# Float32r in place of float32: the gate products over stacked rounded parts, the folds of the modulations in two passes

## What is computed

```python
mod_ctx = jax.nn.silu(c_ctx) @ w_ada[l] + b_ada[l]            # modulations: 2 rows of 6 * 2048
mod_lat = (jax.nn.silu(c) @ w_ada[l] + b_ada[l])[:, None, :]
...
h = x * (1 + sc1) + sh1
z = h @ w_in
q, k, v, g, a_f, a_b, p = jnp.split(z, [K_OFF, V_OFF, G_OFF, AF_OFF, AB_OFF, P_OFF], axis=-1)
log_a_f = heads(jax.nn.log_sigmoid((a_f @ w_a2[0] + b_a[0]).astype(f32)) / GLA_GATE_TEMP, GLA_DK)
log_a_b = heads(jax.nn.log_sigmoid((a_b @ w_a2[1] + b_a[1]).astype(f32)) / GLA_GATE_TEMP, GLA_DK)
```

## Time and profile before

| | |
|---|---|
| median of 3 runs | 2717.18 us (2715.28 to 2717.35) |
| the profiled execution, its own time | 2721.88 us |
| its span, first to last instruction | 2720.1 us |
| PE busy | 2643.3 us (97%) |
| DVE, ACT, POOL busy | 1424.9, 898.4, 652.8 us (52%, 33%, 24%) |
| stage with gates and folds | about 150 to 610 us of the span |
| mean granted TensorE clock | 0.991 of full speed |

### The profile page before, as it was taken

The page is one execution under the profiler, slowest core; times in us unless marked ns, Lnnn a source line. Parts: engine busy times, 40 slices in busy tenths (PEclk is TensorE's granted clock), DMA queues, the critical chain, the costliest instruction groups (busy, mean ns, idle before and its releaser), DMA issues.

```text
span 2720.1 us, 37395 instructions
## 1 busy us (share of the span) xinstructions
PE 2643.3 (97%) x16040; PEld 2354.7 (87%) x16040; DVE 1424.9 (52%) x1680; ACT 898.4 (33%) x940; POOL 652.8 (24%) x218
## 2 busy tenths in 40 slices
PE   5999999998999999999999999999999999999997
PEld 3787877797988879999999999999999888888875
DVE  5323232346576457655555545555566354444578
ACT  4333333332311154333333333333333333333343
POOL 0000000000000001344443444344434333333440
PEclk9999999999999989999999999999999999999998
DMA  9775757422463142332233323332334645464566
GB/s 378 281 277 209 272 207 255 153 90 91 176 218 118 64 159 80 108 108 88 93 108 108 96 86 106 108 103 84 101 108 158 239 174 213 174 213 166 208 231 233
DMA packets 179384, 438.11 MB, mean 161 GB/s; under 512 B 9980, under 2 KB 25732, under 8 KB 173076
## 3 DMA queue, kind: packets, MB, share of 16 engines
q1 hardware_dynamic: 176916, 430.48, 45.4%
q10 hardware_dynamic: 2304, 5.24, 0.5%
HBM read 401.83 MB, written 33.85 MB: 160 GB/s over the span
## 4 chain that ended last, share of the span: by engine, by line
PE 62%; DVE 11%; DMA 10%; POOL 10%; issue 4%; ACT 3%; SPq 0%; POOLq 0%; ACTq 0%; DVEq 0%
PE ps L2355 6%; PE ps L2356 6%; PE ps L2357 6%; DMA raw_w<-w_gu_b 5%; PE ps L2278 5%; PE ps L2280 5%; PE ps L2279 5%; PE ps L2031 5%; PE ps L2033 5%; PE ps L2032 5%; POOL raw_w L945 3%; PE ps L2011 3%; DVE w_lo L1666 3%; POOL low L942 2%; POOL raw_w L948 2%
## 5 line engine op out<-in xcount | busy, mean ns | idle before, releaser
L1666 DVE TENSOR_TENSOR w_lo<-raw_w,w_hi 128x1024 fp32r<-128x1024 f32 x264 | 336.6, 1276 | 297.6 <-ACT w_hi L1210 294.7
L1210 ACT ACTIVATE w_hi<-raw_w 128x1024 fp32r<-128x1024 f32 x264 | 270.1, 1054 | 601.0 <-POOL raw_w L951 368.9
L2278 PE MATMUL ps<-x_hi,w_hi 128*128 128x320 f32 x1408 | 435.7, 309 | 1.0 <-DVE w_lo L1666 0.7
L2279 PE MATMUL ps<-x_lo,w_hi 128*128 128x320 f32 x1408 | 435.1, 309 | 0.0
L2280 PE MATMUL ps<-x_hi,w_lo 128*128 128x320 f32 x1408 | 435.1, 309 | 0.0
L942 POOL TENSOR_TENSOR low<-raw_w 128x1024 f32<-128x1024 f32 x41 | 103.7, 2528 | 1098.8 <-DMA raw_w<-w_gu_b 1058.7
L1801 DVE TENSOR_TENSOR x_lo<-low,x_hi 128x2560 fp32r<-128x2560 f32 (+2 forms) x55 | 221.3, 4027 | 262.6 <-ACT x_hi L1303 262.6
L2355 PE MATMUL ps<-w_hi,x_hi 128*128 128x512 f32 x880 | 343.8, 391 | 7.7 <-DVE w_lo L1932 2.8
L2356 PE MATMUL ps<-w_lo,x_hi 128*128 128x512 f32 x880 | 343.1, 390 | 0.0
L2357 PE MATMUL ps<-w_hi,x_lo 128*128 128x512 f32 x880 | 342.9, 390 | 0.0
L2278 PE MATMUL ps<-low_r,w_hi 128*128 128x320 f32 x1072 | 333.0, 311 | 1.5 <-DVE w_lo L1666 1.5
(11 more groups left out here) (238 smaller groups left out, 4362.9 us busy)
## 6 DMA issues: line engine op xcount, KB each, us to landing
raw_w<-w_gu_b SPq DMA_DIRECT2D x180, 512.0 KB, 5.6
low<-w_ada SPq DMA_DIRECT2D x68, 1024.0 KB, 6.9
raw_w<-w_down SPq DMA_DIRECT2D x55, 1024.0 KB, 5.2
low<-hidden_scratch SPq DMA_DIRECT2D x33, 1280.0 KB, 6.0
raw_w<-w_in_b SPq DMA_DIRECT2D x33, 1024.0 KB, 9.1
x_raw<-w_ada SPq DMA_DIRECT2D x25, 1024.0 KB, 15.2
raw_w<-w_out SPq DMA_DIRECT2D x16, 1024.0 KB, 5.1
hidden_scratch<-high SPq DMA_DIRECT2D x44, 320.0 KB, 5.9
```

What stands on the lines that cost most here:

```text
L1210: nc.scalar.activation(weight(0, w), src, ACT.Copy).then_inc(prod_hi, 1)
L1666: nc.vector.tensor_tensor(weight(1, n), src, weight(0, n).bitcast(F32), ALU.subtract).then_inc(prod_split, 1)
L2278: mm(out, wh, version(v, 0, k), start=first and k == 0, stop=False)
L2279: mm(out, wh, version(v, 1, k), start=False, stop=False)
```

## The change

Gates: unit 0's 32 columns are copied twice on POOL beside themselves, so that the unit's product gives `a` on 96 partitions. ACT writes it rounded to float32r (96 rows), and once more unrounded for the middle 32..64 rows; DVE turns rows 32 to 63 into the remainder (`a_split`). The weights `wa` are loaded three times (three DMAs a head) onto 96 partitions of `high`, ACT rounds them (`wa_parts`, line 1165 of the new file), DVE makes the last 32 rows the remainder. So one float32r product over 96 rows is rounded times rounded, remainder times rounded and rounded times remainder. The row of ones is gone; the bias is loaded once as columns (one DMA of 128 x 8 single elements) and added in the DVE minimum and in the ACT absolute value.

Folds: ACT writes the copy of bank 3 rounded, DVE makes the remainder (a new item on DVE for `adarow`), and each fold is two float32r passes with `group_sum_r`. PE waits for `ada_rest` (the remainder) where it waited for `ada_row`.

The core of the diff:

```diff
-        for at, item in ((1, ("wa", h, 0)), (2, ("state", h, 0)), ...
+        for at, item in ((1, ("wa", h, 0)), (3, ("wa_parts", h, 0)), (2, ("state", h, 0)), ...
@@ SyncE
             elif kind == "wa":
                 if a:
-                    x, k = USES["gate", a - 1, 1][0]
-                    sp.wait_ge(filled[x], k + 1)
-                sp.dma_start(low[0:K_ARR, L_WA:L_WA + 256].rearrange("p (d c) -> p d c", d=2),
-                             wa2[:, :, a * DK:(a + 1) * DK]).then_inc(wa_in, 16)
+                    sp.wait_ge(wa_split, a)
+                else:
+                    sp.dma_start(cols(C_BA, 2 * HEADS).rearrange("p (d h) -> p d h", d=2),
+                                 wa2[2 * RANK].rearrange("d (h p) -> p d h", p=P),
+                                 allow_slow_non_contiguous=True).then_inc(ba_in, 16)
+                for i in range(3):
+                    dst = high[32 * i:32 * i + 32, H_WA:H_WA + 256].rearrange("p (d c) -> p d c", d=2)
+                    sp.dma_start(dst, wa2[0:2 * RANK, :, a * DK:(a + 1) * DK]).then_inc(wa_in, 16)
@@ GpSimd
+        pool.wait_ge(raw_in[0], 16)
+        first_unit = raw_w[:, 0, :].rearrange("p (k c) -> p k c", k=KT)
+        for i in (1, 2):
+            nc.gpsimd.tensor_copy(first_unit[:, :, 32 * i:32 * i + 32],
+                                  first_unit[:, :, 0:32]).then_inc(a_copied, 1)
@@ ScalarE
+            if u == 0:
+                act.wait_ge(a_copied, 2)
...
             if kind == "a":
                 for half in range(2):
-                    ins = nc.scalar.activation(half_of(low[0:2 * RANK, L_AT:L_AT + T], half),
-                                               ps[0:2 * RANK, main_bank(n, half), 0:HALF], ACT.Copy)
+                    nc.scalar.activation(half_of(low_r[0:3 * 2 * RANK, L_AT:L_AT + T], half),
+                                         ps[0:3 * 2 * RANK, main_bank(n, half), 0:HALF], ACT.Copy)
+                for half in range(2):
+                    ins = nc.scalar.activation(half_of(low[2 * RANK:4 * RANK, L_E:L_E + T], half),
+                                               ps[2 * RANK:4 * RANK, main_bank(n, half), 0:HALF], ACT.Copy)
...
+            elif kind == "wa_parts":
+                act.wait_ge(wa_in, 48 * (a + 1))
+                if a:
+                    x, k = USES["gate", a - 1, 1][0]
+                    act.wait_ge(filled[x], k + 1)
+                nc.scalar.activation(low_r[0:3 * 2 * RANK, L_WA:L_WA + 256], high[0:3 * 2 * RANK, H_WA:H_WA + 256],
+                                     ACT.Copy).then_inc(wa_rounded, 1)
...
-                nc.scalar.activation(high[:, H_ROW:H_ROW + 512], ps[:, 3, :], ACT.Copy).then_inc(ada_row, 1)
+                nc.scalar.activation(row_parts[0], ps[:, 3, :], ACT.Copy).then_inc(ada_row, 1)
@@ VectorE
+            elif kind == "adarow":
+                if a:
+                    xx, kk = USES["adacol" if ADA[(a - 1) // 4][1] == "col" else "adasum", a - 1, 0][0]
+                    dve.wait_ge(filled[xx], kk + 1)
+                dve.wait_ge(ada_row, a + 1)
+                nc.vector.tensor_tensor(row_parts[1], ps[:, 3, :], row_parts[0].bitcast(F32),
+                                        ALU.subtract).then_inc(ada_rest, 1)
...
+            elif kind == "wa_parts":
+                rows = slice(4 * RANK, 6 * RANK)
+                dve.wait_ge(wa_rounded, a + 1)
+                nc.vector.tensor_tensor(low_r[rows, L_WA:L_WA + 256], high[rows, H_WA:H_WA + 256],
+                                        low_r[rows, L_WA:L_WA + 256].bitcast(F32),
+                                        ALU.subtract).then_inc(wa_split, 1)
...
-                nc.vector.tensor_scalar(lo(L_LA, T), pair(x), 0.0, None, ALU.min).then_inc(gate_split, 1)
+                dve.wait_ge(ba_in, 16)
+                nc.vector.tensor_scalar(lo(L_LA, T), pair(x), gate_bias(a, b), 0.0, ALU.add,
+                                        ALU.min).then_inc(gate_split, 1)
@@ TensorE
                 elif b == 0:
-                    pe.wait_ge(ada_row, a)
+                    pe.wait_ge(ada_rest, a)
...
             elif kind == "gate":
                 x, k = uses[0]
-                pe.wait_ge(zin_evac, 1)
-                pe.wait_ge(ones_row, 1)
-                pe.wait_ge(wa_in, 16 * (a + 1))
+                pe.wait_ge(a_split, 1)
+                pe.wait_ge(wa_split, a + 1)
                 take(x, k)
                 for c, n in ((0, 512), (512, T - 512)):
-                    ins = pair_mm(x, n, c, low[0:K_ARR, L_WA + b * P:L_WA + (b + 1) * P],
-                                  low[0:K_ARR, L_AT + c:L_AT + c + n], True, True)
+                    ins = pair_mm(x, n, c, low_r[0:6 * RANK, L_WA + b * P:L_WA + (b + 1) * P],
+                                  low_r[0:6 * RANK, L_AT + c:L_AT + c + n], True, True)
...
             elif kind == "adasum":
                 x, k = uses[0]
-                pe.wait_ge(ada_row, a + 1)
+                pe.wait_ge(ada_rest, a + 1)
                 take(x, k)
-                mm(pair(x, 512)[0:2, :], group_sum, high[:, H_ROW:H_ROW + 512],
-                   start=True, stop=True).then_inc(filled[x], 1)
+                mm(pair(x, 512)[0:2, :], group_sum_r, row_parts[0], start=True, stop=False)
+                mm(pair(x, 512)[0:2, :], group_sum_r, row_parts[1], start=False, stop=True).then_inc(filled[x], 1)
             elif kind == "adacol":
...
-                    ins = mm(pair(x, 8)[:, 2 * kk:2 * kk + 2], high[:, H_ROW + kk * P:H_ROW + (kk + 1) * P],
-                             group_sum, start=True, stop=True)
+                    for i in range(2):
+                        ins = mm(pair(x, 8)[:, 2 * kk:2 * kk + 2], row_parts[i][:, kk * P:(kk + 1) * P],
+                                 group_sum_r, start=i == 0, stop=i == 1)
```

More of the change, by code:

```diff
@@ L92 @@
 C_COND = C_SUM + 2
-N_PERM = C_COND + 32 * KT
+C_BA = C_COND + 32 * KT
+C_SUMR = C_BA + 2 * HEADS
+N_PERM = C_SUMR + 2
 L_Q, L_K, L_V, L_LA, L_E, L_E3 = 0, 640, 1280, 2560, 3200, 3840
@@ L159 @@
 H_SCORE, H_ROW = 0, 2048
-H_CARRY = 640
-H_RC = 960
+H_CARRY = 320
+H_WA = 640
+H_RC = 896
+H_REST = 1536
 F_A, F_B, F_SIL, F_HF = 0, 640, 960, 1280
@@ L199, in make_schedule @@
         after_k = 4 * (where["k", h, 0] + 1)
-        for at, item in ((1, ("wa", h, 0)), (2, ("state", h, 0)), (2, SLOT), (4, ("gate", h, 0)), (4, SLOT),
+        for at, item in ((1, ("wa", h, 0)), (3, ("wa_parts", h, 0)), (2, ("state", h, 0)), (2, SLOT), (4, ("gate", h, 0)), (4, SLOT),
                          (6, ("vT", h, 0)), (6, SLOT), (6, ("cum", h, 0)), (8, ("score", h, 0)), (8, SLOT),
@@ L334, in backbone @@
     w_down_v = w_down.rearrange("(g k p) (nb c) -> nb g p k c", g=N_DG, k=DG, p=P, nb=4)
-    perm = nc.alloc_sbuf_tensor("perm", [P, N_PERM], F32)
+    with nc.sbuf_tensor("perm", [P, N_PERM], F32) as perm:
+        pass
+    perm_r = nc.alloc_sbuf_tensor("perm_r", [P, N_PERM], F32R)
     with nc.sbuf_tensor("x_raw", [P, 2 * KT * T], F32) as x_raw:
@@ L348, in backbone @@
     low_r = nc.alloc_sbuf_tensor("low_r", [P, LOW], F32R)
-    high = nc.alloc_sbuf_tensor("high", [P, HIGH], F32)
+    with nc.sbuf_tensor("high", [P, HIGH], F32) as high:
+        pass
+    high_r = nc.alloc_sbuf_tensor("high_r", [P, HIGH], F32R)
     ps = nc.alloc_psum_tensor("ps", [P, 8, 512], F32)
@@ L385, in backbone @@
     group_sum = cols(C_SUM, 2)
+    group_sum_r = perm_r[:, C_SUMR:C_SUMR + 2]
+    row_parts = [high_r[:, c:c + 512] for c in (H_ROW, H_REST)]
     mod_col = cols(C_MOD, 64).rearrange("p (s k c) -> p s k c", s=2, c=2)
@@ L397, in backbone, with gate_bias @@
     carry = high[:, H_CARRY:H_CARRY + HALF]
+    def gate_bias(h, d):
+        return cols(C_BA + HEADS * d + h, 1)
     mean_square = cols(C_STAT + 40, TT)
@@ L530, in backbone @@
     drained = [sem("pair_a_drained"), sem("pair_b_drained")]
-    ones_row = sem("ones_row")
+    a_copied = sem("a_copied")
+    a_split = sem("a_split")
+    ba_in = sem("ba_in")
+    wa_rounded = sem("wa_rounded")
+    wa_split = sem("wa_split")
     wa_in = sem("wa_in")
@@ L563, in backbone @@
     ada_row = sem("ada_row")
+    ada_rest = sem("ada_rest")
+    sums_rounded = sem("sums_rounded")
     row_out = sem("row_out")
@@ L972, in split_in @@
             act.wait_ge(raw_in[s], 16 * (u // 2 + 1))
-            if u == 2:
+            if u == 0:
+                act.wait_ge(a_copied, 2)
+            elif u == 2:
                 act.wait_ge(turned, 4 * TT)
@@ L1009, in evac_turned_a @@
                                      ACT.Copy).then_inc(turned_out_a, 1)
+        act.wait_ge(sums_ready, 1)
+        nc.scalar.activation(group_sum_r, group_sum, ACT.Copy).then_inc(sums_rounded, 1)
         for t in range(TT):
@@ L1128, in _ @@
                 act.wait_ge(gate_split, g + 1)
-                nc.scalar.activation(e, pair(x), ACT.Abs).then_inc(drained[x], 1)
+                nc.scalar.activation(e, pair(x), ACT.Abs, bias=gate_bias(a, b)).then_inc(drained[x], 1)
                 act.wait_ge(drained[x], k + 1)
```

(7 more changed lines are left out.)

6 lines of the change are left out of this document (3 added, 3 removed).

## The result

The changed kernel takes 2721.95 us (median of 22 runs, 2717.69 to 2726.14), the kernel before 2717.62 us (22 runs, 2713.28 to 2722.18). I had forecast 2712.3 us, 2707.0 to 2717.5.

A forecast was written before the change was run, and what follows sets the result against it. Between 150 and 600 us TensorE's own work was taken as the bound. Gates save 1.9 us of 7.4 after waits, row folds 3.0, column folds nothing: 4.9 us off 2717.2 gives 2712.3 us, range 2707.0 to 2717.5.

The forecast's parts named there:

- Prices on PE: TensorE cost per step: a gate 0.34 us, saving 0.93; a row fold saves 0.38; a column fold saves nothing.
- My lower end for the column folds: Column folds on TensorE, worst case: passes at 0.15 us cost 0.25 us more a fold, 2.0 in all.
- First gate: PE would wait for the block's remainder on DVE until about 164.0: the gate's saving gone and 0.1 us lost.
- Second and sixth: nothing behind them is close: 0.93 each: Second and sixth gates: no close dependency follows, so each keeps its full saving of 0.93 us.
- Third gate: Second head, first direction: PE waits 0.4 us for `wa`'s remainder, the column fold behind 1.5; PE 1.0 us later than before.
- Fourth gate, costed at 0: The column fold behind already waits 0.47 us for ACT; the saving only lengthens this wait, to 1.4: 0 saved.
- Fifth and seventh: Third and fourth head, first direction: PE waits 0.35 us for `wa`'s remainder, no fold behind: 0.58 us saved each.
- Eighth, costed at 0: PE already waits 2.44 us for pooled tiles behind this gate's scans; the wait becomes near 3.3: 0 saved.
- Costed at nothing: POOL copies, unit 0's extra ACT and DVE work, other fourteen block remainders and bias transfer: taken as hidden, 0 us.
- The bias transfer's upper end of 7.4 us: Bias DMA burst near 135 us: 64 packets per engine at 0.12 us each, costing the kernel some 5 us.
- The smaller estimate there, 0.7 us: Bias DMA: 64 packets at the Trainium skill's roughly 10.5 ns each for tiny transfers.
- a rival at one place, the transposes: Clock behind the last head's transposes wait: stays at 2.4 GHz, 2708.9 us (0.08); low stretch twice as long, 2715.7 (0.1).

The follow-up runs named there:

- the run with the extra matmuls: Changed kernel plus 20 unused float32r matmuls in each of two waits, ahead of the first pooled product and the last head's transposes: 2719.12 us, ratio 0.9996.

## Why the prediction was wrong, point by point

- **Prices on PE: right.** A gate 0.40 us (0.34 forecast); each gate that doesn't wait saves 0.97 to 1.07 where it stands, against 0.93. A row fold's two passes start 0.23 apart, and it saves 0.46 to 0.49 against 0.38. A column fold saves nothing (289.20 to 290.09, 0.89 us, had 0.92). Two-column passes take 0.11 us in both types; the fast weight load that the Trainium skill ("TensorE: Matmul & The Clock Gate", section "Weight-path perf modes") gives to types other than FP32 isn't to be seen in these rows. (My lower end for the column folds, 2.0 us lost, should have been 2.2: 8 x 0.15 less 0.92 is 0.28 a fold.)

```profile
166.96 0.40 PE L2254 MATMUL ps<-high_r,perm_r 128*2 128x512 f32 x1
167.19 0.40 PE L2255 MATMUL ps<-high_r,perm_r 128*2 128x512 f32 x1
...
289.20 1.02 PE L2263 MATMUL ps<-perm_r,high_r 128*128 128x2 f32 x8 [1.61 <-ACT low L1172]
290.09 0.39 PE L2094 MATMUL ps<-x_hi,w_hi 128*128 128x320 f32 x1
```

- **First gate: right.** The wait for the remainder is 0.7 us; gate and row fold together gain 0.3 between 149 and 170 us, forecast 0.28.
- **"Second and sixth: nothing behind them is close: 0.93 each": the first step that failed.** Each gained 1.0 us; the wait of 1.4 us within 16 us behind it took that back, and the saving of the next row fold too. I looked for what touches a gate or a fold, in a list of waits, and a place with 0.11 us of slack has no row there. The question was what ACT and DVE owe PE a unit later. I also read that list too quickly: it isn't true that one wait alone touches a gate or a fold, since a row fold waits 0.9 us for DVE. That wait stayed at 0.9 and the fold kept its saving.
- **Third gate.** The wait's size was right (1.6 against 1.5; +1.1 us against before, in the run with the gates alone too, forecast 1.0). The clock drop behind it added 1.5. **This is the second step that failed: a new wait was priced by its length alone**, here and at the fourth and the eighth gate.
- **Fourth gate, costed at 0.** The wait was forecast at 1.4 and is 1.6. Costs +0.15 with the clock up, +1.7 with the drop.
- **Fifth and seventh: right**, 0.55 and 0.69 against 0.58. Behind a wait of 1.45 us at 585 us, which the kernel before has too, the clock fell in the changed kernel: +1.5.
- **Eighth, costed at 0.** PE waits 3.7 (3.3 forecast), which alone is about even, and the 6.8 us of low clock, most of it in the float32 product behind it, cost 2.9 (4.1 less the 1.2 of the run with the extra matmuls).
- **Costed at nothing** (POOL's copies, the bias transfer, unit 0): no run shows a cost of its own, and the spread of the openings hides one of the order of 1 us. The bias transfer's upper end of 7.4 us was far too high: in the trace of the changed kernel its 4-byte packets took 9 ns each, 0.6 us on each DMA engine. The smaller estimate there, 0.7 us, was the right one.

The sum from 215 to 754 us: my terms there are -0.93 + 1.0 - 0.58 - 0.93 - 0.58 and five row folds, -1.9, together -3.9. The trace says +6.1, so 10.0 are missing. The second and sixth gate, each with its wait and the row fold behind, were to give -2.6 and show +0.2: 2.8. The clock drops at 290, 359, 587 and 618 us cost 1.5 + 1.5 + 1.5 + 2.9 = 7.4. The late start near 306 us is 0.4. The drop at the transposes cost 0.5 less than before, since it began within the wait. Together 10.1. The clock is the larger part. I had it as a rival at one place, the transposes, and named another low stretch only as what would make me wrong; four terms create or lengthen a wait, and none had its price. So the range ended too low, at 2717.5.

What stays open: how often each drop comes. There is one profile of each kernel, and each is one draw. That may be why the times show 4.3 us and not 6.1; it isn't shown.

## What to carry to other kernels

Before a shorter instruction is credited, follow the other engines' chain from the same starting event to the next thing PE needs from it, and write down the slack; a place with 0.1 us of it has no row among the waits. Price a new wait of TensorE with the clock behind it, not only its length. Where such a wait can't be removed, work that fills it can be worth more than the wait.

## What the runs showed of the hardware

- Whether the clock drops behind a wait differs between places and executions. Over the 14 profiles: behind waits of 1.6 us ahead of the column folds of the third and fourth gate it fell 7 times in 10, in the kernels whose wait there is 0 to 0.5 us never in 16 (the run with seven gates moved is left out: its waits of 2.3 us lie ahead of the gates, and it fell behind 2 of 3). Waits that look alike did otherwise: behind those of 0.9 to 1.4 us at 233 and 501 us it never fell (12 waits), behind that of 1.45 us near 582 us 5 times in 14, behind that of 1.6 us near 635 us 4 times in 14. At the pooled product it fell 5 times in 5 after 3.7 us, once in 2 after 2.4 us, never in 7 after less than 0.8 us. Ahead of the last head's transposes, after 3.2 us, 10 times in 10, and never in 4 with the wait filled.
- Behind waits of 1.5 to 2.4 us the drop begins 0.9 to 2.4 us after the wait has ended, while PE is busy again (290 to 294 us above), and lasts 3.4 us. At the waits of 3.2 and 3.7 us it mostly begins in their last 0.3 to 1.5 us (twice 1.7 us behind them), and lasts 6.8 or 10.2 us.
- A float32r fold with weights of 128 by 128 and two moving columns is no cheaper than the float32 one: 8 passes in 0.89 us against 0.92, and the record of a weight load is 191 ns long in both.
- A bias operand made the 640-column minimum on DVE 0.06 us (0.82 to 0.88) and the absolute value on ACT 0.09 us (0.70 to 0.80) longer.
- The 1024 packets of 4 bytes of the bias transfer took 9 ns each: 0.6 us on each of the 16 DMA engines.
